# Norm totals as two rounded products with ones, and the rotary key turned later, in a one-core fp32 encoder block

## What is computed

```python
def rmsnorm(x, g):
    x32 = x.astype(jnp.float32)
    y = x32 * lax.rsqrt(jnp.mean(x32 * x32, axis=-1, keepdims=True) + RMS_EPS)
    return (y * g.astype(jnp.float32)).astype(x.dtype)

u = rmsnorm(h, g_mix[i])
z = u @ w_in[i]
qa, ka, va, cq, ckv, kr, ga, gb = jnp.split(z, SPLITS, axis=-1)
...
qb = (rmsnorm(cq, q_a_norm[i]) @ w_q_b[i]).reshape(b, s, N_HEADS_B, QK_DIM_B)
kv = (rmsnorm(ckv, kv_a_norm[i]) @ w_kv_b[i]).reshape(b, s, N_HEADS_B, NOPE_DIM_B + V_DIM_B)
k_pe = axial_rope(kr[:, :, None, :], ang_rb, ang_cb)
...
h = h + merged @ w_o[i]
gu = rmsnorm(h, g_ffn[i]) @ w_gate_up[i]
...
h = h + (jax.nn.silu(g_) * u_) @ w_down[i]
e = rmsnorm(p[i] @ w_ple_proj[i], g_ple_post[i])
gate = jax.nn.sigmoid(rmsnorm(h, g_ple[i]) @ w_ple_gate[i])
h = h + gate * e
return rmsnorm(h, g_final)
```

## Time and profile before

| | us |
|---|---|
| median of three runs | 2807.18 |
| lowest, highest | 2807.03, 2807.37 |
| the profiled execution | 2806.76 |
| its span, first to last instruction | 2805.0 |
| PE busy | 2787.2 (99%) |
| DVE busy | 1229.7 (44%) |
| ACT busy | 893.6 (32%) |
| POOL busy | 213.4 (8%) |

### The profile page before, as it was taken

How to read it: one execution, slowest core, us unless ns; L and a number is a source line. 1 busy time by engine, 2 the same in 40 slices (tenths; PEclk the granted TensorE clock), 3 DMA queues, 4 the chain that set the end, 5 groups by cost and what they waited for, 6 DMA issues and landing times.

```text
span 2805.0 us, 32071 instructions
## 1 busy us (share of the span) xinstructions
PE 2787.2 (99%) x12532; PEld 2303.6 (82%) x12532; DVE 1229.7 (44%) x1300; ACT 893.6 (32%) x1115; POOL 213.4 (8%) x118
## 2 busy tenths in 40 slices
PE   9999999999999999999999999999999999999998
PEld 7888888888888888888888888888888888888887
DVE  6555555355654444333333333334333333336635
ACT  5344444335544232322222222222222222224433
POOL 0000000010000211000000000000000000004432
PEclk9999999999999999999999999999999999999999
DMA  6333333333233643333333333333333333332332
GB/s 213 98 98 98 105 98 105 98 90 105 94 116 113 225 135 97 105 98 98 96 94 95 96 97 97 97 97 97 97 94 95 96 97 97 97 97 93 95 98 98
DMA packets 278911, 295.20 MB, mean 105 GB/s; under 512 B 9024, under 2 KB 261056, under 8 KB 278720
## 3 DMA queue, kind: packets, MB, share of 16 engines
q1 hardware_dynamic: 274352, 285.90, 32.7%
q10 hardware_dynamic: 4496, 8.44, 0.8%
HBM read 277.53 MB, written 16.78 MB: 105 GB/s over the span
## 4 chain that ended last, share of the span: by engine, by line
PE 97%; DVE 1%; ACT 1%; DMA 1%; issue 0%; POOL 0%; SPq 0%; DVEq 0%; ACTq 0%; POOLq 0%
PE ps L380 32%; PE ps L382 31%; PE ps L381 31%; PE ps L449 1%; PE ps L438 0%; DMA raw<-w_o 0%; DVE w_lo L1196 0%; ACT w_hi L752 0%; DVE emb L1667 0%; PE ps L404 0%; PE ps L416 0%; DMA raw<-w_in 0%; PE ps L495 0%; DVE r L1231 0%; PE ps L497 0%
## 5 line engine op out<-in xcount | busy, mean ns | idle before, releaser
L380 PE MATMUL ps<-r,w_hi 128*128 128x512 f32 x3824 | 1493.8, 391 | 3.0 <-DVE w_lo L1196 2.5
L382 PE MATMUL ps<-r,w_lo 128*128 128x512 f32 x3824 | 1488.2, 389 | 0.0
L381 PE MATMUL ps<-r,w_hi 128*128 128x512 f32 x3824 | 1487.9, 389 | 0.0
L1196 DVE TENSOR_TENSOR w_lo<-raw,w_hi 128x1024 fp32r<-128x1024 f32 x480 | 602.2, 1255 | 1374.6 <-ACT w_hi L752 1373.4
L752 ACT ACTIVATE w_hi<-raw 128x1024 fp32r<-128x1024 f32 x484 | 512.6, 1059 | 1530.8 <-PE ps L382 1518.4
L380 PEld LDWEIGHTS ps<-r,w_hi 128*128 128x128 f32 x3824 | 717.7, 188 | 157.4 <-issue 6.6
L382 PEld LDWEIGHTS ps<-r,w_lo 128*128 128x128 f32 x3824 | 717.7, 188 | 150.0
L381 PEld LDWEIGHTS ps<-r,w_hi 128*128 128x128 f32 x3824 | 717.9, 188 | 148.9 <-issue 1.2
L1721 POOL TENSOR_TENSOR tmp<-tmp 128x1024 f32<-128x1024 f32 x22 | 52.6, 2392 | 1339.0 <-DVE tmp L1208 1339.0
L1559 DVE TENSOR_TENSOR res<-ps,res 128x1024 f32<-128x1024 f32 x96 | 116.8, 1217 | 2.9 <-PE ps L382 2.9
L1208 DVE TENSOR_TENSOR tmp<-ps,rstd 128x1024 f32<-128x1024 f32 x69 | 84.0, 1218 | 1.6 <-PE ps L382 1.5
(11 more groups left out here) (122 smaller groups left out, 995.2 us busy)
## 6 DMA issues: line engine op xcount, KB each, us to landing
raw<-w_gu SPq DMA_DIRECT2D x176, 512.0 KB, 3.6
raw<-w_in SPq DMA_DIRECT2D x108, 512.0 KB, 3.8
raw<-w_dn SPq DMA_DIRECT2D x88, 512.0 KB, 3.4
raw<-w_o SPq DMA_DIRECT2D x32, 512.0 KB, 3.5
raw<-w_pg SPq DMA_DIRECT2D x32, 512.0 KB, 3.5
gates<-tmp ACTq DMA_DIRECT2D x16, 512.0 KB, 2.8
raw<-w_a SPq DMA_DIRECT2D x16, 512.0 KB, 3.7
res<-gates SPq DMA_DIRECT2D x16, 512.0 KB, 5.3
```

The source lines that it names most:

```text
L380: mm(out, hi, x[:, 0, :], start=start, stop=False)
L381: mm(out, hi, x[:, 1, :], start=False, stop=False)
L382: return mm(out, lo, x[:, 0, :], start=False, stop=stop)
L1196: tt(w_lo[:, j % HL], raw[:, j], w_hi[:, j % HL], ALU.subtract).then_inc(w_lo_done, 1)
```

## The change

Six totals of norms are made otherwise. ACT rounds the tile of summed squares to fp32r (`sum_split`), DVE subtracts for the remainder (`sum_low`), and PE multiplies the rounded ones with each of the two parts and adds them in PSUM. The parts have a new tile `sum_r`; norm 5, whose total is made beside norm 4's, uses `r1[:, 7]`. The rounded ones, until now made behind `recip(0)`, are made in front of the first total. In the lists of ACT and DVE the new instructions of norms 0, 1 and 2 stand behind the rounding of the piece that PE uses right after the total; those of norms 3, 4 and 5 stand behind the rounding of the third piece of the group in front of the total. The rotary key is turned not in front of `wlo(N_LAT + 10)` but behind `wlo(N_LAT + 13)` and the four latent tiles, in front of `latent_query(2)`.

```diff
+        sum_r = sb("sum_r", [P, 2, SEQ], F32R)
...
+        sum_hi, sum_lo = sem("sum_hi"), sem("sum_lo")
...
+        SUM_PARTS = [sum_r[:]] * 5 + [r1[:, 7]]
+        SQUARES = [16, 20, 24, 40, 56, 72]
...
             def total(norm, bank):
 
-                pe.wait_ge(acc_done, [16, 20, 24, 40, 56, 72][norm])
-                mm(ps[:, bank, :], ones, sums(norm), start=True, stop=True).then_inc(tot_done, 1)
+                if norm == 0:
+                    pe.wait_ge(ones_set, 1)
+                pe.wait_ge(sum_lo, norm + 1)
+                mm(ps[:, bank, :], ones_r[:], SUM_PARTS[norm][:, 0, :], start=True, stop=False)
+                mm(ps[:, bank, :], ones_r[:], SUM_PARTS[norm][:, 1, :], start=False, stop=True).then_inc(tot_done, 1)
 
             def head_total(m):
-                if isinstance(m, int) and m == 0:
-                    pe.wait_ge(ones_set, 1)
...
+            def sum_split(norm):
+                act.wait_ge(acc_done, SQUARES[norm])
+                copy(SUM_PARTS[norm][:, 0, :], sums(norm)).then_inc(sum_hi, 1)
...
             whi(6, 2)
+            sum_split(0)
             whi(7, 3)
             root(0, 7, 0, D)
...
             whi(N_LAT + 10, 2)
+            sum_split(1)
             root(1, 6, 2, LORA)
...
             whi(N_LAST_GATES + 2, 2)
+            sum_split(2)
             root(2, 7, 1, LORA)
...
-            four(N_FF)
+            whi(N_FF + 2, 2)
+            sum_split(3)
+            for j in range(1, 4):
+                whi(N_FF + 2 + j, (2 + j) % 4)
             root(3, 3, 0, D)
...
                 if g not in (1, 7):
                     whi(b + 2, 2)
+                if g == 0:
+                    sum_split(4)
+                    sum_split(5)
...
+            def sum_low(norm):
+                dve.wait_ge(sum_hi, norm + 1)
+                tt(SUM_PARTS[norm][:, 1, :], sums(norm), SUM_PARTS[norm][:, 0, :], ALU.subtract).then_inc(sum_lo, 1)
...
             wlo(6, 2)
+            dve.wait_ge(mats_in, 16)
+            nc.vector.tensor_copy(ones_r[:], ones).then_inc(ones_set, 1)
+            sum_low(0)
             wlo(7, 3)
             recip(0, 0, 7, 0, D)
-            dve.wait_ge(mats_in, 16)
-            nc.vector.tensor_copy(ones_r[:], ones).then_inc(ones_set, 1)
...
-            rotate(10, res[:, 12:13, :], 2, res[:, 6:7, :], res[:, 7:8, :], ROPE_B // 2, 24, OP_KR)
             wlo(N_LAT + 10, 2)
+            sum_low(1)
             recip(1, 1, 6, 2, LORA)
             wlo(N_LAT + 11, 3)
             for k in range(4):
...
                 if k % 2:
                     wlo(N_LAT + 12 + k // 2, k // 2)
+            rotate(10, res[:, 12:13, :], 2, res[:, 6:7, :], res[:, 7:8, :], ROPE_B // 2, 24, OP_KR)
             latent_query(2)
...
             wlo(N_LAST_GATES + 2, 2)
+            sum_low(2)
             recip(2, 2, 7, 1, LORA)
...
-            four(N_FF)
+            wlo(N_FF + 2, 2)
+            sum_low(3)
+            for j in range(1, 4):
+                wlo(N_FF + 2 + j, (2 + j) % 4)
             recip(3, 3, 3, 0, D)
...
                     wlo(N_PLE + 4 * g + 2 + j, (2 + j) % 4)
+                    if g == 0 and j == 0:
+                        sum_low(4)
+                        sum_low(5)
```

## The result

| | us |
|---|---|
| before, median of 20 executions | 2807.03 (2806.36 to 2807.50) |
| changed kernel, median of 20 | 2810.57 (2809.59 to 2811.55) |
| ratio, with its 95% interval | 1.0013 (1.0007 to 1.0019) |
| profiled execution of the changed kernel | 2810.83, span 2808.9 |

The changed kernel is 3.5 us slower, 0.13%. The interval excludes 1, and all of it lies within the 0.2% that the prediction named as what a measurement tells. Forecast were 2810.5 and a span of 2808.3.

A forecast was written before the change was run, and what follows sets the result against it. PE was taken to bound the kernel, with DVE setting the pace only around the query latent. Totals -2.5, key +4.3 and clock +1.5 gave +3.3 us, so 2810.5 against the median, range 2808.1 to 2812.2.

The forecast's parts named there:

- What bounds the kernel: PE, busy 2787.2 of 2805.0 us; only time in its own stream or its stops moves the end.
- The totals, -2.5 us: On PE at six norms: a rounded pair instead of an fp32 total saves 0.42 us each, 2.5 in all.
- The added waits, nothing: ACT's rounding and DVE's subtraction before each total end before PE arrives: cost 0, at most 0.7 us.
- The stop of 0.7: At norm 1, with the rotary key before the subtraction, PE would wait 0.7 us for the total's low part.
- The key, +4.3 us: Rotary key before the query latent's emptying, in a chain without slack, lengthens PE's stop by 4.3 us; other end 6.2.
- The clock, +1.5 us: PE's 5.0 us stop near the query latent likely lowers the granted clock once, costing 1.5 us, between 0 and 2.6.
- My upper end, 2.6: Largest price of one clock fall: 16 warm-up products lose 2.6 us while PE comes up from rest.
- The stop without a fall of the clock, 2809.0: Rival: PE's stop at the query latent comes, the clock stays up; +1.8 us, 2809.0; chance 0.30.
- the rotation keeps 6.2 us: Rival: rotary key as slow in its new place as in its old, clock at full price; +6.3 us, 2813.5; chance 0.06.
- the chain has slack: Rival: unseen slack around the query latent, so no added PE stop; only the totals count, 2804.7; chance 0.07.
- the pair saves nothing: Rival: at the totals, rounded products cost PE what fp32 did; +4.3 us without the clock, 2811.5; chance 0.02.

The follow-up runs named there:

- The kernel with the key in the gap: Changed kernel with the rotary key turned two pieces later, where DVE waits five us for PE: 2804.27 us against 2807.20 for the kernel before.
- the key in its old place: Changed kernel with the rotary key back in front of the low part of the piece behind the second total, totals still rounded: 2805.42 us against 2807.20.
- the two pairs with PE kept busy: 18 unread products added in PE's stop: to the changed kernel, 2808.97 us; to the kernel before with the rotary key late and fp32 totals, 2811.68 us.
- the sum alone late: Changed kernel with only the rotary key's last instruction in the new place, all its products in the old one: 2805.24 us against 2807.17.
- the half key's run: Changed kernel with the rotary key split, two sine products and the final add in the new place, the rest in the old: 2807.92 us against 2807.13.

## Why the prediction was right

- **What bounds the kernel.** Held. The microseconds put into PE's stream or its waits came out one to one, to within some 0.3; ACT's six copies and DVE's six subtractions were free but for one case.
- **The totals, -2.5 us.** Held in kind, too small by a few tenths. The kernel with the key in the gap has -2.9 in the median. The stretches of the table that hold nothing but totals have 0.44, 0.46 and 0.83 for four of the six, which is 2.6 for all. Behind an fp32 total PE goes on at 0.232 a step, not at 0.227, for eight steps: from the product ahead (1172.92) to the ninth one behind the total are 2.95 us before (its start is 1175.87), and 2.50 after (1178.15 to 1180.65). I had read no further than the second product and found 0.42; with the tail it is 0.45, or 2.7 for six. The last 0.2 or 0.3 is within the scatter of medians.
- **The added waits, nothing.** Held. No total waits for its low part; norm 1 had 2.0 us to spare where I had 1.7, as POOL's two adds took 2.72 us without the key beside them, not 3.42. The stop of 0.7 that I gave for norm 1 with the key in its old place was measured as 0.68.
- **The key, +4.3 us.** Held: 4.25 in the profile, and by experiment 4.27 in its stretch, 4.5 and 4.7 in the medians of the two pairs with PE kept busy. Two choices carried this term. One was to ask of the chain whether it had slack: it had none. The other was the length: 4.26 of another rotation instead of 6.2 of this one. The sine products took 2.82 or 2.83 without POOL beside them, in the changed kernel and in five others, and 4.79 or 4.80 in the three where POOL's adds ran at the same time (before, the key in its old place, the sum alone late). By the Trainium skill, page SBUF — State Buffer, section Who interferes with whom, they block each other; the runs agree, with 2.82 against 4.80, and POOL gains too, 2.72 against 3.42. The 1.2 us per product of the prediction is a mean of unequal ones: in the trace of before the first and the last took 0.68, and the two in the middle 1.67 each, ending 0.54 us behind the end of POOL's first and of its second add.
- **The clock, +1.5 us.** Held in kind; 1.8 and 1.9 in the medians, 1.46 and 2.87 in two profiled executions. My upper end, 2.6, was drawn from warm-up products, and one execution lay above it. I had let part of the low stretch fall into the stop and so be free; in the changed kernel only 0.25 us of it did. What I had not seen either is that the price differs from one execution to the next, with the stop the same. And the row that I held against a fall, the clock still up across 2.16 us, says less than I took from it: PE had two products left behind that stop, and the half key's run shows a fall that comes only when PE is at work again.
- **The rivals.** The stop without a fall of the clock, 2809.0, is what was measured once PE was kept busy (2808.97). That the rotation keeps 6.2 us, that the chain has slack, that the pair saves nothing: each ruled out by a row or a run above.
- **The sum.** -2.9 + 4.6 + 1.8 = +3.5. These are differences along a row of kernels from before to changed, so they add up to the result by their making; that the key has 4.5 and the clock 1.9 with fp32 totals too is the independent part. Mine was -2.5 + 4.3 + 1.5 = +3.3. All three terms were short by 0.3 or 0.4 in size, and of different signs, so the forecast of 2810.5 for 2810.57 is partly luck; 0.3 us is what each term is good for.

## What to carry to other kernels

Where one engine is 99% busy, look for the few microseconds in which another engine sets its pace, and move nothing into that stretch: six cheap instructions there cost more than six totals gave. Before an instruction is moved for the sake of one wait, list what stands behind its new place until the bound engine's next wait; here an idle time of five microseconds lay two pieces further on. And a stop of the matrix engine has two prices, its length and the slow products behind it; in the stops of up to 1.2 us only the first was paid here, in those of 4.7 both, and at 2.75 the second in most executions.

## What the runs showed of the hardware

- The granted clock fell to 0.50 at stops of PE of 4.7 us (at about 597.15, 0.25 us before PE's next product) and of 2.75 (0.5 us behind it), and stayed at 1.00 at those of 0.5, 0.66 and 1.14. It was still 1.00 at the end of the one of 2.16, but there PE had only two products left. Behind stops of one length, 7 steps were slow in one execution and 14 in another, 0.43 us instead of 0.23. 18 products of no use in the stop avoided it and cost nothing. The Trainium skill, page TensorE: Matmul & The Clock Gate, section Why this matters for your kernels, warns of such gaps; these runs agree, and put the price at 1.5 to 2.9 us for each.
- Behind an fp32 product with a 128x512 operand the rounded products took 0.232 a step for eight steps, against 0.227 behind a rounded pair. After a stop of PE the same slower steps are seen (0.23 to 0.24 behind 600.55 in the changed kernel). So they may come from the break in the stream and not from the fp32 form; no run here separates the two.
- A DVE product of 32 partitions and two inputs in SBUF took 0.68 us alone (0.71 from one start to the next). Of four beside two POOL adds, two took 1.67 each and two 0.68 (before). The adds took 1.29 each alone (changed kernel) and 1.72 and 1.56 beside them.
